# First expert pass: a half of each score copied by ScalarE, the halves added three tiles behind, the choice spread over more tiles

## What is computed

```python
def peer_ffn(h, wq, subkeys, u_tab, v_tab):
    q = (h @ wq).reshape(bsz, s, PEER_HEADS, 2, PEER_KEY_DIM // 2)
    s1 = jnp.einsum('bshd,kd->bshk', q[:, :, :, 0], subkeys[0]).astype(f32)
    s2 = jnp.einsum('bshd,kd->bshk', q[:, :, :, 1], subkeys[1]).astype(f32)
    v1, i1 = lax.top_k(s1, PEER_TOPK)
    v2, i2 = lax.top_k(s2, PEER_TOPK)
    cand = (v1[..., :, None] + v2[..., None, :]).reshape(bsz, s, PEER_HEADS, n_cand)
    ...
    best, pos = lax.top_k(cand, PEER_TOPK)
    eidx = jnp.take_along_axis(cidx, pos, axis=-1)
    gate = jax.nn.softmax(best, axis=-1).astype(h.dtype)
    ...
        act = jax.nn.gelu(jnp.einsum('td,tkd->tk', hx, u_tab[ex]))
        return jnp.einsum('tk,tkd->td', act * gx, v_tab[ex])
```

## Time and profile before

| | before |
|---|---|
| median of 3 runs | 3828.37 us (3826.17 to 3831.27) |
| the profiled execution | 3846.25 us, its span 3844.5 us |
| TensorE busy | 3440.2 us (89%) |
| VectorE busy | 2697.3 us (70%) |
| ScalarE busy | 1246.8 us (32%) |
| GpSimd busy | 451.0 us (12%) |
| HBM over the span | 225 GB/s |

### The profile page before, as it was taken

The page is one execution under the profiler, slowest core; times in us unless marked ns, Lnnn a source line. Parts: engine busy times, 40 slices in busy tenths (PEclk is TensorE's granted clock), DMA queues, the critical chain, the costliest instruction groups (busy, mean ns, idle before and its releaser), DMA issues. The chain is left out here.

```text
span 3844.5 us, 43044 instructions
## 1 busy us (share of the span) xinstructions
PE 3440.2 (89%) x17195; PEld 2708.1 (70%) x17195; DVE 2697.3 (70%) x3331; ACT 1246.8 (32%) x1339; POOL 451.0 (12%) x419
## 2 busy tenths in 40 slices
PE   7989878998899999999999799987988998999898
PEld 5756556798799998878777586576844776443576
DVE  6855778799999986778878646555446445795564
ACT  3323233334344534444444333213311101200333
POOL 0011111101111121232322000020000211000000
PEclk8888888999899999999999899998999999899899
DMA  9973477657799998999999453206552112553563
GB/s 361 379 240 123 127 268 283 238 197 272 272 335 350 355 360 304 382 367 376 378 376 370 163 196 101 77 6 209 189 185 93 29 44 61 150 152 121 190 231 142
DMA packets 294599, 870.08 MB, mean 226 GB/s; under 512 B 33584, under 2 KB 108436, under 8 KB 242432
## 3 DMA queue, kind: packets, MB, share of 16 engines
q1 hardware_dynamic: 257616, 670.64, 49.8%
q0 software_dynamic: 34320, 190.40, 13.1%
q10 hardware_dynamic: 2464, 6.29, 0.4%
HBM read 820.22 MB, written 46.38 MB: 225 GB/s over the span
## 5 line engine op out<-in xcount | busy, mean ns | idle before, releaser
L2899 ACT ACTIVATE expert_w_high<-expert_w 128x2048 fp32r<-128x2048 f32 x256 | 490.7, 1917 | 746.5 <-DMA expert_w<-in_peer_v_dram 300.1
L2807 PE MATMUL bank<-h_halves,expert_w_high 128*128 128x384 f32 x2048 | 628.4, 376 | 72.9 <-DVE expert_w_low L2476 72.0
L2476 DVE TENSOR_TENSOR expert_w_low<-expert_w,expert_w_high 128x2048 fp32r<-128x2048 f32 x256 | 585.1, 2286 | 148.9 <-ACT expert_w_high L2899 146.9
L294 DVE TENSOR_TENSOR weights_low<-weights,weights_high 128x1024 fp32r<-128x1024 f32 (+4 forms) x288 | 338.1, 1177 | 304.9 <-ACT weights_high L277 301.5
L2808 PE MATMUL bank<-h_halves,expert_w_low 128*128 128x192 f32 x2048 | 526.7, 257 | 0.0
L2807 PEld LDWEIGHTS bank<-h_halves,expert_w_high 128*128 128x128 f32 x2048 | 402.4, 196 | 85.7 <-DVE expert_w_low L2476 85.4
L277 ACT ACTIVATE weights_high<-weights 128x1024 fp32r<-128x1024 f32 (+4 forms) x288 | 293.6, 1022 | 475.4 <-PE bank L322 385.4
L2808 PEld LDWEIGHTS bank<-h_halves,expert_w_low 128*128 128x128 f32 x2048 | 409.1, 200 | 0.0
L2876 PE MATMUL bank<-expert_w_high,gated_acts_halves 128*128 128x512 f32 x512 | 203.0, 397 | 21.5 <-DVE expert_w_low L2476 21.4
L3154 PE MATMUL bank<-s_gates_w,x_rows 128*128 128x512 f32 x448 | 202.7, 613 | 0.1
L2878 PE MATMUL bank<-expert_w_high,gated_acts_halves 128*128 128x512 f32 x512 | 201.7, 394 | 0.0
(11 more groups left out here) (721 smaller groups left out, 6834.9 us busy)
## 6 DMA issues: line engine op xcount, KB each, us to landing
expert_w<-in_peer_u_dram SPq DMA_DIRECT2D x128, 1024.0 KB, 6.8
expert_w<-in_peer_v_dram SPq DMA_DIRECT2D x128, 1024.0 KB, 9.4
weights<-in_ada_w_dram SPq DMA_DIRECT2D x88, 512.0 KB, 9.2
weights<-in_w_out_dram SPq DMA_DIRECT2D x32, 1024.0 KB, 13.6
weights<-in_w_in_dram SPq DMA_DIRECT2D x32, 960.0 KB, 9.7
weights<-in_w_in_dram SPq DMA_DIRECT2D x32, 928.0 KB, 9.7
weights<-in_w_in_dram SPq DMA_DIRECT2D x56, 512.0 KB, 7.0
s_gates_w<-in_w_in_dram SPq DMA_DIRECT2D x56, 512.0 KB, 3.7
```

The lines of the kernel that those rows point to most:

```text
L294: dve.tensor_tensor(self.low[:, u % self.UNITS_HELD, :, 0:n], self.buf[b][:, k:k + self.UNIT, 0:n], self.high[:, u % self.UNITS_HELD, :, 0 ...
L2476: dve.tensor_tensor(wl[:, n % RING, :], w_sb[:, n % RING, :], wh[:, n % RING, :], ALU.subtract).then_inc(wl_ready, 1)
L2807: pe.matmul(o[:, 0:2 * DENSE], uh[:, b, k, :], acts.both[:, k, :, 0:DENSE], start=(k == 0), stop=False)
L2899: act.activation(wh[:, n % RING, :], w_sb[:, n % RING, :], ACT.Copy).then_inc(wh_ready, 1)
```

## The change

ScalarE gets a new instruction in each of the 128 tiles: it copies columns 192 to 383 of the score bank into half_scores, a buffer of two in unused columns of act_area. It stands ahead of high(n+3) and, from tile 2, waits until VectorE has added tile n-2. VectorE's add becomes a tensor_tensor of the bank's first 192 columns and the copy; it waits for the copy and is done in step n+3. The gelu of a group moves by one tile, and so does SP's store. The quota of the choice is 2.8 until the first tokens are listed and 1.9 after that.

```diff
-    TILE_TIME = 2.6
+    TILE_TIME, TILE_TIME_BESIDE_DOTS = 2.8, 1.9
...
+        half_scores = act_area[:, 2 * STEP * DENSE:2 * (STEP + 1) * DENSE].rearrange("p (b t) -> p b t", b=2)
+        half_copied = m.sem("half_scores_copied")
...
-                    score_ring.free(dve.tensor_reduce(act_sb[:, g % 2, t, :], view(bank[:, 0:1], [[1, DENSE], [DENSE, 2]]), AX_X, ALU.add))
+                    dve.wait_ge(half_copied, n + 1)
+                    score_ring.free(dve.tensor_tensor(act_sb[:, g % 2, t, :], bank[:, 0:DENSE], half_scores[:, n % 2, :], ALU.add))
...
                     if n >= 2:
                         low(n)
-                        add_halves(n - 2)
+                    if n >= 3:
+                        add_halves(n - 3)
...
-                        while spent < TILE_TIME:
+                        time = TILE_TIME if plan.listed is None else TILE_TIME_BESIDE_DOTS
+                        while spent < time:
...
+                add_halves(TILES - 3)
                 add_halves(TILES - 2)
                 add_halves(TILES - 1)
...
-                    done = n - 7
+                    done = n - 8
...
                     act.wait_ge(score_ring.filled, n + 1)
+                    if n >= 2:
+                        act.wait_ge(score_ring.emptied, n - 1)
+                    act.activation(half_scores[:, n % 2, :], score_ring.banks[n % 4][:, DENSE:2 * DENSE], ACT.Copy)\
+                        .then_inc(half_copied, 1)
                     high(n + RING)
-                    if t == 0 and g:
+                    if t == 1 and g:
                         gelu(g - 1)
```

## The result

| | before | after |
|---|---|---|
| median | 3828.0 us (3826.17 to 3831.27) | 3801.03 us (3796.81 to 3803.97) |
| ratio to before | | 0.9919, 95% interval 0.9907 to 0.9931 |
| the profiled execution | 3846.25 us | 3800.45 us |

The account below looks back on a forecast made before the run. VectorE was taken to pace the first expert pass up to its tail, TensorE the tail. The terms +9.9 + 2 - 31.9 - 0.7 + 0.3 = -20.4 us gave 3808 us on the median, range 3798 to 3820.

Parts of the forecast that it names:

- The add and the copy: Each tile: VectorE's add falls from 550 to 350 ns, saving 0.20 us; ScalarE's new copy takes some 340 ns, hidden.
- VectorE's count for the part: From low(4) to low(103) instead of low(96): seven more low halves, five more dots, cheaper adds; +9.9 us.
- 2 us more of waits for DMA: Gate tiles: needing 364 GB/s instead of 347, loads behind a 2 MB gate store have no slack; +2 us.
- rival (a): Gate tiles: the transfers bind and the rate stays at 347 GB/s, so 3820 us; chance 0.18.
- The start and the end: Tiles 2 and 3 do one add fewer and a cheaper one, -0.7 us; copy ahead of the last add, +0.3.
- The last store of activations and the fetch behind it: End of the pass: store one SP step later, fetch starts 4 to 5 us later, hidden by the second pass; nothing.
- Seven tiles of the tail: Seven tiles pass from the TensorE-paced tail to the VectorE part, at 4.55 us each; -31.9 us.
- Steps moved in the tail: Tail stalls on SP's queue at the gate and modulation row stores move seven tiles at unchanged price; 0, bounds -5 and +9.
- Rival (b): The tail's stalls merge or shorten, no added DMA waits, TensorE less behind at the tail's start; 3798 us; chance 0.13.
- Rival (c): Slower: SP's stop at step 115 for the modulation row makes loads 116 to 120 late, 30 us; 3838 us; chance 0.05.
- Rival (d): The new add costs the same as the reduce, so only the spread of the choice works; 3828 us; chance 0.04.
- Rival (e): The handshake with VectorE paces ScalarE, putting 43 us of copies on the path; 3851 us; chance 0.02.

Follow-up runs that it names:

- after_again: The changed kernel once more, unchanged, for a second trace; median 3800.86 us, ratio to before 0.9933.
- add_alone: The changed kernel with both quotas of the choice at the old 2.6, so the copy, cheap add and later gelu alone; 3817.16 us, ratio to before 0.9963.
- copy_and_reduce: The changed kernel, but VectorE still reduces all 384 elements; copy and waits stay, the copy's data unused; 3824.79 us, ratio to before 0.9985.
- before_no_stop: The kernel before the change, but SP doesn't stop until the modulation row is stored; 3830.9 us, ratio 0.9998.
- before_rows_later: The kernel before the change, with the first two fetches of expert rows for the second pass held until tile 125; 3830.04 us, ratio 1.0.
- dots_end_124: The kernel before the change with the dots spread up to tile 124 in place of 118; 3826.66 us, one run.

## Why the prediction was right in its way and wrong in its size

- **The add and the copy**: forecast 350 and some 340 ns, measured 349 and 328. The nearest row of another shape and a slope of 1.04 ns an element were enough.
- **VectorE's count for the part**: +9.9 forecast (its four terms as printed add to 9.8; the difference is rounding), +10.1 measured. Right, and right again for each half of the change.
- **2 us more of waits for DMA** (bounds 0 and 13.9): not seen. VectorE idled 2.2 and 4.6 us in the part, before 4.2 and 3.6: 2 us less in the first pair of traces, 1 more in the second. The gate tiles moved 362 GB/s, 364 by the count, so rival (a), a rate stuck at 347, is refuted. The Trainium skill's figure beside it ("DMA: Bandwidth & Descriptors", section Bandwidth, about 358 GB/s for a core) did not bind: 362 is just above it, and the 382 of the second pass well above. The forecast read that figure wrongly. The section gives it as a core's share with both cores of the HBM domain streaming, and this program runs on one core.
- **The start and the end**: the pass ahead of the part went from 33.3 to 32.1 us, -1.2 where -0.7 was forecast. The copy ahead of the last add was forecast at +0.3 and lies in the tail: the last add starts 5.2 us after the last tile's first matmul, before 4.8.
- **The last store of activations and the fetch behind it**: the fetch was forecast to start 4 to 5 us later against the end of the pass, at no cost. Before, it started 23.0 us after the last add (1541.20, 1518.20), now 28.3 us (1507.58 and 1479.26), 5.3 later:

```profile
1507.58 2.67 POOL L2774 DMA_INDIRECT expert_act<-in_peer_v_dram,own_list  x1 [88.83 <-DMA expert_acts<-expert_act]
```

  The second pass took 597.9 and 601.1 us after, 603.1 and 591.9 before: no cost that can be seen.
- **Seven tiles of the tail**: -31.9 forecast, and 171.0 to 131.4 is -39.6, by the second pair 172.1 to 132.0, -40.1. The forecast failed here, in the step "Steps moved in the tail", "Taken: no change; bounds -5 (two stalls in one) and +9". The tiles themselves are right; what lies over them went from 25.4 to 17.6 us. Of these 7.8 us, 6.7 are stalls (steps 18.7 to 11.9; 19.8 to 12.6 in the second pair) and 1.4 is TensorE's earlier start in the tail, less 0.4 for the later last add. The stalls did not all keep their price. The one behind the 2 MB store did (waits of 4.0 and 5.9 us before, 4.9 and 5.4 after); those at 109, 111 and 119, 11.9 us with the low clock behind them, shrank to 4.4.
- **Why the bound was too small**: I priced a stall at TensorE's idle time only. The clock lost in the tail fell from 10.1 to 3.4 us, more than the idle time did (10.9 to 8.1); 1.7 of it is the spell at the tail's start, which hangs on no stall of the tail. With 7.8 us in the tail and the 2 us of waits that did not come, the sum is 9.8 larger: -30.2 us, against -32.7 and -29.6 in the two pairs of traces and -31 (26 to 36) by the ratio. Rival (b), stalls that merge or get shorter, came nearest, with a price of 10 us in all (its parts as printed add to 11, so 3797 in place of 3798). By the medians 7 of them came, by the ratio 11: the stalls gave 6.7 where it allowed 5, and TensorE's earlier start 1.4 where it allowed 4. Its reason was not what happened. The later gates met their loads as before, and the row store and tile 119 shared no stall. No other term was off by more than 4 us.
- **Rival (c), the row store lands in the crowd**: no. SP stops at 1401.29 for 9.9 us, where 9 were forecast, and the waits of TensorE behind it are all 1.1 us or less (1.5 in after_again).
- **Rival (d)**, an add as dear as the reduce: refuted by its row, and by add_alone, 0.9963.
- **Rival (e), the handshake**: refuted by after itself, and by copy_and_reduce. ScalarE's waits for VectorE's adds came many and short as forecast (43 waits, 113.3 us, the longest 4.9) and cost nothing that can be measured.

What stays open. Where the extra 8 us are is shown by two pairs of traces; that they are loads meeting fetches is argued from the times of issue and landing, and from how the waits moved with the gate store and the dots. Which fetch delays which load was not isolated, so why those loads came earlier after the change is open. The ratio of add_alone (-14 us) is also smaller than its trace (pass -23.8), and before_no_stop's pass was 5.7 us shorter in its trace with a ratio of 0.9998: so 5 us in one trace should not be believed before a ratio shows them.

## What to carry to other kernels

In a stretch that one engine paces, the start to start count of its instructions forecast the change in its work to a microsecond; its waits moved by some us from trace to trace. The helper engine's copy was free here, where the helper waits for others most of the time. Where TensorE paces, a stall is worth its idle time and the low clock behind it, and moving work by a few tiles moves the stalls: price them as removable and as new ones, not as fixed. A large store ahead of a prefetch load is worth cutting into pieces, one to a load: the kernel that did so had no large wait, though it held back two fetches as well.

## What was not expected of the hardware

The granted clock falls to 0.5 of full speed, 1.2 of 2.4 GHz, at quite short gaps of TensorE in otherwise dense work. In the tails of the two traces of before and the two of after, all eight gaps of 2.6 to 5.9 us have 3.4 to 10.2 us at 0.5 at them or behind them, and the gaps of 1.5 us and less have none of their own. By the steps from tile to tile a gap of 2.6 us thus cost 4.5 us, one of 2.8 cost 5.7. The tails of the other kernels show that the length of a gap doesn't settle it: one of 2.6 us (before_rows_later, tile 118) had no low clock, one of 1.8 (dots_end_124, tile 123) had 3.4 us of it. The other surprise is how little the DMA queue minded more load: 362 GB/s through the gate tiles (359 in after_again), with VectorE idle 2.2 and 4.6 us over the part, where it was 4.2 and 3.6 at 347.
